# A class of 120 columns, and two of four down chunks in three half-precision passes for items of 120 and 112 columns, in the expert stage of a hybrid decoder layer

## What is computed

```python
logits = xt @ w_router + b_router                  # 1024 tokens, 32 experts
top_vals, top_idx = lax.top_k(logits, 4)
gates = softmax(top_vals)
def expert_block(x_blk, e):
    gu = x_blk @ w_gate_up[e] + b_gate_up[e]       # 1024 -> 2048
    g = minimum(gu[:, :1024], 7.0); u = clip(gu[:, 1024:], -7.0, 7.0)
    act = (u + 1.0) * (g * sigmoid(1.702 * g))
    return act @ w_down[e] + b_down[e]             # 1024 -> 1024
out = segment_sum(y * gate, token)
```

## Time and profile before

| | |
|---|---|
| median of 3 runs | 1878.76 us (1878.45 to 1881.33) |
| the profiled execution | 1882.29 us, its span 1880.5 us |
| PE busy | 1800.9 us (96%), 21814 matmuls |
| DVE busy | 1402.1 us (75%) |
| ACT busy | 1231.7 us (65%) |
| granted TensorE clock | 0.982 mean |
| DMA | 479.07 MB, mean 255 GB/s, 362 to 377 GB/s over the last ten slices but one |

### The profile page before, as it was taken

The page is one execution under the profiler, slowest core; times in us unless marked ns, Lnnn a source line. Parts: engine busy times, 40 slices in busy tenths (PEclk is TensorE's granted clock), DMA queues, the critical chain, the costliest instruction groups (busy, mean ns, idle before and its releaser), DMA issues.

```text
span 1880.5 us, 53844 instructions
## 1 busy us (share of the span) xinstructions
PE 1800.9 (96%) x21814; PEld 1650.7 (88%) x21814; DVE 1402.1 (75%) x2678; ACT 1231.7 (65%) x1649; POOL 411.4 (22%) x304
## 2 busy tenths in 40 slices
PE   8999998998987999999999999999999999999996
PEld 7777765666876999999999999999999999999996
DVE  5553637775258888888888899999889877757755
ACT  6565327873114777777777788877777776656654
POOL 4000000001003212111112332333122224434433
PEclk9999999999988999999999999999999999999998
DMA  5211101004438988889999999999999999999994
GB/s 153 56 44 39 30 24 45 2 1 142 142 120 295 369 293 308 304 302 320 325 320 322 328 313 343 344 336 345 373 375 365 372 372 374 377 375 372 362 370 134
DMA packets 251408, 479.07 MB, mean 255 GB/s; under 512 B 17312, under 2 KB 38096, under 8 KB 251264
## 3 DMA queue, kind: packets, MB, share of 16 engines
q1 hardware_dynamic: 231040, 443.59, 64.9%
q0 software_dynamic: 20256, 33.94, 7.6%
HBM read 466.96 MB, written 47.19 MB: 273 GB/s over the span
## 4 chain that ended last, share of the span: by engine, by line
PE 50%; issue 6%; DVE 6%; ACT 4%; DMA 2%; DVEq 0%; SPq 0%; POOLq 0%; ACTq 0%; POOL 0%
PE E_p_d L2254 9%; PE E_p_g L2242 5%; PE E_p_g L2245 5%; PE E_p_g L2244 5%; PE E_p_u L2242 5%; PE E_p_u L2245 5%; PE E_p_u L2244 5%; PE E_p_d L2242 3%; PE E_p_d L2245 3%; PE E_p_d L2244 3%; DVE E_w_lo L1996 3%; DMA E_w_st<-in_w_down 2%; PE E_p_t L2180 2%; PE E_p_t L2195 2%; ACT E_w_hi L1869 2%
## 5 line engine op out<-in xcount | busy, mean ns | idle before, releaser
L1996 DVE SCALAR_TENSOR_TENSOR E_w_lo<-E_w_st,E_w_hi 128x2048 f16<-128x2048 f32 x336 | 767.2, 2283 | 31.7 <-ACT E_w_hi L1869 30.5
L1869 ACT ACTIVATE E_w_hi<-E_w_st 128x2048 f16<-128x2048 f32 x336 | 639.0, 1907 | 20.3 <-PEq L1325 16.8
L2242 PE MATMUL E_p_u<-E_x_hi,E_w_hi 128*128 128x128 f16 (+9 forms) x2048 | 366.9, 222 | 1.5 <-DVE E_w_lo L1996 1.4
L2244 PE MATMUL E_p_g<-E_x_lo,E_w_hi 128*128 128x128 f16 (+9 forms) x2048 | 366.9, 222 | 0.5 <-issue 0.5
L2242 PE MATMUL E_p_g<-E_x_hi,E_w_hi 128*128 128x128 f16 (+9 forms) x2048 | 366.9, 222 | 0.0
L2245 PE MATMUL E_p_g<-E_x_hi,E_w_lo 128*128 128x128 f16 (+9 forms) x2048 | 366.9, 222 | 0.0
L2245 PE MATMUL E_p_u<-E_x_hi,E_w_lo 128*128 128x128 f16 (+9 forms) x2048 | 366.8, 222 | 0.0
L2244 PE MATMUL E_p_u<-E_x_lo,E_w_hi 128*128 128x128 f16 (+9 forms) x2048 | 366.8, 222 | 0.0
L1799 POOL DMA_INDIRECT out<-E_y_rows,E_idx_out x66 | 152.6, 2312 | 488.0 <-ACT E_y_rows L1887 467.1
L2242 PE MATMUL E_p_d<-E_a_hi,E_w_hi 128*128 128x160 f16 (+6 forms) x1024 | 210.6, 231 | 6.9 <-DVE E_a_lo L2090 3.5
L2245 PE MATMUL E_p_d<-E_a_hi,E_w_lo 128*128 128x160 f16 (+6 forms) x1024 | 210.5, 231 | 0.0
(11 more groups left out here) (419 smaller groups left out, 3487.2 us busy)
## 6 DMA issues: line engine op xcount, KB each, us to landing
E_w_st<-in_w_gate_up SPq DMA_DIRECT2D x130, 2048.0 KB, 13.5
E_w_st<-in_w_down SPq DMA_DIRECT2D x64, 2048.0 KB, 18.7
A_w_st<-in_w_in SPq DMA_DIRECT2D x20, 512.0 KB, 4.0
A_x_rows<-in_x SPq DMA_DIRECT2D x8, 512.0 KB, 7.9
C_x_res<-in_x SPq DMA_DIRECT2D x8, 512.0 KB, 4.7
x_rows<-C_x SPq DMA_DIRECT2D x8, 512.0 KB, 5.2
out<-C_x SPq DMA_DIRECT2D x8, 512.0 KB, 5.9
h_rows<-C_h SPq DMA_DIRECT2D x8, 512.0 KB, 4.5
```

The costliest lines, as they stand in the source:

```text
L1869: act.activation(w_hi[r][:], staged(c), ACT.Copy, scale=SW).then_inc(hi_s if c < NG else down_hi_s, 1)
L1996: dve.scalar_tensor_tensor(out=w_lo[r][:], in0=staged(c), scalar=SW, in1=w_hi[r][:], op0=ALU.mult, op1=ALU.subtract, accum_out=total[:, c: ...
L2242: pe.matmul(o_, wh, hi[:, k, 0:w], start=h == 0 and k == 0, stop=False, skip_group_check=True)
L2244: pe.matmul(o_, wh, lo[:, k, 0:w], start=False, stop=False, skip_group_check=True)
```

## The change

Two constants take the place of one. `HALVES`, from which on an item is wide, goes from 128 to 112; `SLIM` = 128 takes over its other part, up to which only two of four down chunks are split and the small buffers `a_slim`, `a_slim_hi`, `a_slim_lo` are used. `WIDTHS` gets a class of 120 between 128 and 112. So the items with 119, 119 and 117 tokens run with 120 columns in place of 128, and the five of 112 columns become wide. The tables of stage D that have a row for each class grow from 12 x 32 to 13 x 32.

```diff
-WIDTHS = (256, 192, 184, 176, 168, 160, 152, 144, 136, 128, 112, 96)
+WIDTHS = (256, 192, 184, 176, 168, 160, 152, 144, 136, 128, 120, 112, 96)
 NV = len(WIDTHS)
-HALVES = 128
+HALVES = 112
+SLIM = 128
...
         def n_split(w):
-            return (NP if w > HALVES else NP // 2) if halves(w) else 0
+            return (NP if w > SLIM else NP // 2) if halves(w) else 0
         def parts_of(w):
-            return (a_hi, a_lo) if w > HALVES else (a_slim_hi, a_slim_lo)
+            return (a_hi, a_lo) if w > SLIM else (a_slim_hi, a_slim_lo)
...
                     def activated_hi(j):
...
-                        src = up[j % 2][:, :, 0:w] if w > HALVES else a_slim[:, 2 * j:2 * j + 2, 0:w]
+                        src = up[j % 2][:, :, 0:w] if w > SLIM else a_slim[:, 2 * j:2 * j + 2, 0:w]
...
-                        to = up[j % 2][:, :, 0:w] if halves(w) and w > HALVES else (
+                        to = up[j % 2][:, :, 0:w] if halves(w) and w > SLIM else (
...
                     def activated_lo(j):
...
-                        src = up[j % 2][:, :, 0:w] if w > HALVES else a_slim[:, 2 * j:2 * j + 2, 0:w]
+                        src = up[j % 2][:, :, 0:w] if w > SLIM else a_slim[:, 2 * j:2 * j + 2, 0:w]
```

## The result

The change takes 1887.07 us in the median of five runs (1880.58 to 1888.42) against 1878.76 (1877.91 to 1881.97, five runs): ratio 1.0033, interval 1.0017 to 1.005. Slower, and by more than the 0.2% that can be told. The ratio is that of the means of all runs and comes to 6.2 us; the two medians lie 8.3 us apart. Further down too a ratio need not be the quotient of the medians beside it. The profiled execution of the change is the quickest of its five: 1880.58, span 1878.8. So its trace has to be read with care, and the first run of the experiments takes a second one.

What follows compares the result with a forecast made beforehand. TensorE, DVE and the loads were taken to stand close together, with DVE and PE arriving together ahead of down at 128 columns. Terms +0.3 - 1.5 + 0.3 + 0.35 + 6.0 = +5.5 us gave 1884.3 us, range 1876.0 to 1889.0.

Steps and rivals of the forecast that it cites:

- TensorE's own work: Down chunks moved from f32 to half precision and columns cut to 120: TensorE relieved of 17.9 us in all.
- DVE ahead of down: DVE's chain before down sets its start at 23.02 us (112) and 23.21 (120); TensorE stands still 2.35 and 1.3 us.
- Down: Down chunks to item end: items of 112 +0.1 us each, +0.3 for five; of 120 -0.5 each, -1.5 for three.
- Tables: Stage D's tables get 32 elements more in nine or so instructions: +0.3 us, between 0 and 0.5.
- One class more: Extra issue on ACT ahead of the table load in a class's first item: +0.35 us, between 0 and 0.7.
- The clock: New 2.35 us stops at 112 columns halve TensorE's clock in four of five items, 1.5 us each: +6.0 us.
- 6.8 us long: Upper bound on the clock's price at 112 columns: five falls of this length, 5 x 3.4 = 17 us.
- Loads: An item's 13.5 MB take 35.8 us at 377 GB/s, just under the item; changed load order on SP costs 0.
- The clock holds: Rival: stops at 112 columns cause no clock fall, so -0.5 us, 1878.3 us; chance 0.34.
- DVE does not hold TensorE: Rival: TensorE's 17.9 us gain arrives, 1861 us, or partly, 1868 to 1875; chance 0.10 (DVE or loads give way).
- Loads come late: Rival: first items of 96 columns wait for a passed load, +5 us, 1883.3 without a clock fall; chance 0.06 alone.

Runs made afterwards that it cites:

- run 4: The change with the stop ahead of down filled by idle matmuls, 9 at 112 columns and 4 at 120: 1882.94 us, ratio 0.9999 to the kernel before.
- run 1: The changed kernel timed and profiled again, no edit: 1886.4 us, ratio 1.0025 to the kernel before.
- run 3: The change without the class of 120 columns, items of 112 still wide: 1888.27 us, ratio 1.0026 to the kernel before.
- run 5: The change with item-loop weight loads bringing only half of each slot, the rest stale: 1885.53 us, ratio 1.0027 to the kernel before.
- run 6: The change with one half-precision down chunk instead of two in items of 112 columns: 1879.19 us, ratio 0.9996 to the kernel before.
- run 7: The change with third `activated_lo` ahead of a low part on DVE and `y_bias(0)` ahead of `next_hi(0)` on ACT, up to 128 columns: 1885.51 us, ratio 1.0012.
- run 10: The change with one half-precision down chunk at 112 columns and the last wide item's loads in narrow order: 1882.43 us, ratio 1.0002 to the kernel before.
- run 2: The change with only the class of 120 columns, items of 112 staying narrow: 1880.95 us, ratio 0.9995 to the kernel before.
- run 9: The change with one half-precision down chunk at 112 columns and item-loop loads bringing half of each slot: 1875.65 us, ratio 0.9974 to the kernel before.
- run 8: The change with only the class of 120 columns, plus five idle matmuls in the stop at 136 columns: 1879.75 us, ratio 0.9997 to the kernel before.
- run 11: The change with one half-precision chunk at 112, last wide item's loads in narrow order, five idle matmuls at 136 columns: 1882.11 us, ratio 0.9997.

## Why the prediction was right

Slower was the likeliest case, 1884.3 was forecast and 1887.07 came; the range of 1876.0 to 1889.0 holds it. The forecast was +5.5 us; by the ratio the change costs 6.2, by the medians 8.3. By the steps:

- *TensorE's own work*, 17.9 us: in the windows PE is busy for 2.47 us less in an item of 112 (35.80 to 33.33) and 1.59 less in one of 120 (36.54 to 34.95), 5 x 2.47 + 3 x 1.59 = 17.1. The page's 18.5 also holds other stages' clocks. The f32 chunk at 112 columns costs what the earlier trace rows gave, 37.6 us over 320 records. Right.
- *DVE ahead of down*: down was to start at 23.02 us (112) and 23.21 (120); it starts at 23.01 to 23.02 and 23.20. The stop at 112 columns was put at 2.35; it is 2.19 (2.52 in the first item), since the transposes end 20.83 us into the item and not at 20.67. At 120 it was put at 1.3 and is 1.10 to 1.12. Right, and the row it turned on was the earlier trace rows.
- *Down*: item of 112 without a fall 35.9 forecast, 35.78 measured; of 120, 36.2 forecast, 36.27 measured. The wait for ACT ahead of down chunk 2 is 0.25, near the 0.20 it was taken at. So +0.1 each is in truth -0.05 each (35.83 before).
- *Tables*: forecast +0.3. `D_kind` takes 591 instead of 557 ns, and from it to `D_start` it is 5.2 instead of 4.9 us, so 0.3 for that stretch alone.
- *One class more*: +0.35 forecast in the class's first item. It came in the first item of 112 (36.12 in run 4, against 35.79 behind it) while the first of 96 lost it (35.29, 35.51 before). Its place was wrong, and its size in sum 0.33 - 0.22 = 0.1, so 0.25 too high.
- *The clock*: 1.5 us a fall in four of five items. A fall costs 37.31 to 37.40 less 35.78, 1.5 to 1.6 us, and over the four profiles of two chunks at 112 columns with the stop open (after, 1, 3, 5) 15 of 20 items had one. This is the term that made the sign, and run 4 shows it by taking it away: 1.0025 (run 1) becomes 0.9999. The mechanism and the price of a fall were worked out; that four of five items would have one was only taken, and that it came so near (3.75 of five on the mean) is luck. So is a part of the support: the prediction let a stop of 1.70 us stand as one that does no harm, on one execution. At the same place, in the same code, four of the later profiles have a fall with stops of 1.53 to 1.92 us. The bound "6.8 us long" was not needed for these stops.
- *Loads*: cost 0, and run 5 agrees for this change. But their pace is 36.1 to 36.3 us an item, and not the 35.8 that was worked out. It could be read before: in the kernel before, one gate slot landed at 1578.21, 1614.46, 1650.72 and 1686.81 in items of 35.83 us. A relief of TensorE in these items could thus only run into that pace later on, whatever DVE did, as runs 6 and 7 show.

What was missed is small: in the profiles of the change and of runs 1, 4 and 10 the first item of 136 columns has a fall too (stops of 1.92, 1.68, 1.53 and 1.76 us, 3.41 us at 1.2 GHz each), in that of the kernel before not (1.70 us there), nor in those of runs 2, 3, 5, 6, 7 and 9 (1.25 to 1.78 us). Its code is the same but for runs 8 and 11, which fill the stop. It costs less than it seems: 41.67 + 39.81 us for the two items of 136 in the change, against 40.30 + 40.45 before, so 0.7. Whether it comes more often with the change stays open; so many profiles don't tell.

The rivals. *The clock holds* is run 4, made by hand: a draw, as priced (1878.3 on 1878.76). *DVE does not hold TensorE* is refuted: a shorter list on DVE (run 6) or another order of it (run 7) does free TensorE, but there the next rival takes over. *Loads come late* was placed rightly (the first item of 96 columns, a slot that has been passed, loads of 20.4 and 19.5 us where some 22 were named), but not for this change. Its price of +5 fits the stop alone (4.4 to 4.9 us); with the fall behind it the item is longer by 6.2 us in run 6 and by 7.9 in run 7. It decides only in kernels whose items are quicker. Even so, run 4's first item of 96 is at 36.14 instead of 35.29, and ACT waits 1.9 us there for a gate slot: without the falls the change stands right at that edge.

The Trainium skill (TensorE: Matmul & The Clock Gate, A second HAM failure mode) tells of short idles between groups of matmuls that make the clock swing and lose throughput. The traces agree, for one stop in some 36 us: stops of 2.2 to 2.5 us were followed by 3.41 us at half clock in 15 of 20 items; the stops of 1.1 us in the items of 120 columns never were.

What stays open is why one item has the fall and the next not, with stops equal to 0.01 us. The falls come in rows once they have begun (four in a row in run 3, each 37.54 or 37.55 us behind the last), which a chance for each item by itself would seldom give. Nor does a fall begin at a fixed distance from its stop: in the change's profile at 1673.00, with the stop ending at 1673.11, and at 1529.64, with the stop ending at 1528.39. So where a stop lies in time may count beside its length; no run moves a stop on purpose, and this is not shown.

## What to carry to other kernels

Count what an engine must do *ahead* of the moment another waits for it, not its busy share: DVE was idle for 11% of the item (31.69 of 35.78 us busy) and still the bound, and TensorE's relief turned into a stop of the same size. A stop of about 2 us in dense matmul work has a price of its own in the clock; fill it, or cut it into pieces, before judging the change that opened it. And where the DMA engines are at a share of 1.04, add up landings from item to item (36.1 us here against items of 35.05, and against 35.83 in the kernel before): as long as they fall back, time won in one class is only lent and is paid in the next.

## What was not expected of the hardware

- A filled stop costs nothing that shows: nine bf16 matmuls of 512 columns (2.11 us) in a stop of 2.2 us left down's start at 23.03 us and made the clock hold in five of five items.
- In stage E the length of a fall went with the stop: 3.41 us at stops of 1.53 to 2.52 us, 6.83 us at those of 2.88, 4.43 and 4.86 us (runs 11, 6, 7), where it began before PE went on. Whether a fall came did not go with the length in the same way: stops of 1.53 us (run 4) had one, and others of 2.2 and 2.36 us (run 11) had none. Ahead of stage B 2.29 us had been followed by 6.8, which is why I had bounded the price by that length.
- In run 6, from 1555 to 1712 us, a load of 2 MB took 12 to 24 us from issue to landing, with the DMA share at 1.04 or 1.05. From item to item the landings of one slot lay 36.1 to 36.3 us apart in the items of 112, in the change (items of 35.8; 36.6 once, behind a fall) and in the kernel before (35.83) as in run 6 (35.05). The time from issue to landing grew with it, by 0.4 us an item in the change and by 1.1 in run 6, so it reads as the queue ahead of a load, and a view of it, item by item, shows the floor before anything waits.
